# The sum of squares of four feed-forwards, as two matmuls of 128 tokens with two weight tiles between them

## The reference, cut to what matters

```python
def rms_norm(x, g):
    y = xf * lax.rsqrt(jnp.mean(xf * xf, axis=-1, keepdims=True) + NORM_EPS)
    return y * g
x = x + 0.5 * swiglu(rms_norm(x, ffn1_norm[l]), w_gate, w_up, w_down)   # silu(x @ w_gate) * (x @ w_up) @ w_down
```

## Time and profile before

| | |
|---|---|
| median of 3 runs | 1090.55 us (1090.24 to 1093.16) |
| the profiled execution's own time | 1091.57 us |
| its span, first to last instruction | 1089.7 us |
| TensorE matmuls busy | 1074.7 us (99%) |
| weight loads busy | 939.6 us (86%), beside the matmuls |
| VectorE, ScalarE, POOL busy | 782.0, 615.4, 186.5 us |
| mean granted TensorE clock | 0.995 |
| transfers | 200.02 MB, 184 GB/s on average |

### The profile page before, as it was taken

One profiled execution on the slowest core, in us unless ns is written; L12 is line 12 of the kernel. 1 busy time (PEld: TensorE's weight loads), 2 busy tenths in 40 slices (PEclk: granted clock), 3 DMA queues, 4 the chain that ended last, 5 costly groups with the idle time before them and its releaser, 6 DMA issues.

```text
span 1089.7 us, 17862 instructions
## 1 busy us (share of the span) xinstructions
PE 1074.7 (99%) x6282; PEld 939.6 (86%) x6282; DVE 782.0 (72%) x1110; ACT 615.4 (56%) x941; POOL 186.5 (17%) x199
## 2 busy tenths in 40 slices
PE   8999999999999999999999999999999999999997
PEld 6888888888788888888888888889988898888886
DVE  6866666798696666668666676787877769666664
ACT  7655544466675555447555445756655556555541
POOL 4411101030021111011111100233210022111100
PEclk9999999999999999999999999999999999999997
DMA  7755555554256555656555554655455646655551
GB/s 281 265 191 191 180 183 179 166 182 142 92 185 205 189 192 175 198 173 209 193 192 188 179 194 153 221 184 193 158 191 193 192 137 215 198 188 190 183 184 39
DMA packets 55571, 200.02 MB, mean 184 GB/s; under 512 B 6304, under 2 KB 6304, under 8 KB 55392
## 3 DMA queue, kind: packets, MB, share of 16 engines
q1 hardware_dynamic: 54576, 196.11, 54.9%
q0 software_dynamic: 512, 2.65, 0.6%
q10 hardware_dynamic: 432, 0.57, 0.2%
HBM read 198.26 MB, written 1.05 MB: 183 GB/s over the span
## 4 chain that ended last, share of the span: by engine, by line
PE 93%; DVE 5%; ACT 1%; DMA 1%; issue 0%; ACTq 0%; DVEq 0%
PE pair L1274 44%; PE pair L1275 22%; PE pair L1296 9%; PE pair L1298 5%; PE pair L1268 3%; PE pair L1270 3%; PE pair L1269 3%; DVE w_lo L790 2%; DVE x_hl L796 1%; DMA x<-x_in 1%; ACT qk_a L623 0%; PE pair L1637 0%; DVE x L807 0%; PE pair L1595 0%; ACT w_hi L429 0%
## 5 line engine op out<-in xcount | busy, mean ns | idle before, releaser
L790 DVE TENSOR_TENSOR w_lo<-w_raw,w_hi 128x1024 fp32r<-128x1024 f32 x369 | 463.1, 1262 | 230.6 <-ACT w_hi L429 229.9
L429 ACT ACTIVATE w_hi<-w_raw 128x1024 fp32r<-128x1024 f32 x369 | 386.1, 1056 | 236.4 <-PE pair L1275 195.4
L1274 PE MATMUL pair<-x_hl,w_hi 128*128 128x512 f32 x1408 | 493.2, 396 | 2.3 <-DVE x_hl L796 1.3
L1275 PE MATMUL pair<-x_hl,w_lo 128*128 128x256 f32 x1408 | 392.6, 279 | 0.0
L1274 PEld LDWEIGHTS pair<-x_hl,w_hi 128*128 128x128 f32 x1408 | 264.0, 187 | 66.1 <-issue 2.1
L1275 PEld LDWEIGHTS pair<-x_hl,w_lo 128*128 128x128 f32 x1408 | 265.2, 188 | 0.1
L1274 PE MATMUL pair<-wide,w_hi 128*128 128x512 f32 x704 | 245.4, 394 | 0.0
L1275 PE MATMUL pair<-wide,w_lo 128*128 128x256 f32 x704 | 196.2, 279 | 0.0
L1274 PEld LDWEIGHTS pair<-wide,w_hi 128*128 128x128 f32 x704 | 132.0, 187 | 30.8
L347 POOL TENSOR_TENSOR wide<-side,wide 128x256 fp32r<-128x256 f32 x88 | 86.4, 982 | 375.8 <-ACT wide L491 375.8
L1275 PEld LDWEIGHTS pair<-wide,w_lo 128*128 128x128 f32 x704 | 132.6, 188 | 0.0
(11 more groups left out here) (191 smaller groups left out, 1059.7 us busy)
## 6 DMA issues: line engine op xcount, KB each, us to landing
w_raw<-stream SPq DMA_DIRECT2D x369, 512.0 KB, 4.2
const<-const_in POOLq DMA_DIRECT2D x1, 1248.0 KB, 8.7
w_raw<-stream SPq DMA_DIRECT2D x4, 256.0 KB, 5.7
out<-x_sq SPq DMA_DIRECT2D x4, 256.0 KB, 2.6
rows<-rows_in POOLq DMA_DIRECT2D x1, 576.0 KB, 10.7
x<-x_in ACTq DMA_DIRECT2D x2, 256.0 KB, 5.7
x<-x_in SPq DMA_DIRECT2D x2, 256.0 KB, 6.8
sgu_w<-sgu_w_in POOLq DMA_DIRECT2D x1, 512.0 KB, 13.7
```

Source lines behind the costliest of these rows:

```text
L429: nc.scalar.activation(w_hi[:, slot, :], w_raw[:, slot, :], ACT.Copy).then_inc(w_hi_done, 1)
L790: nc.vector.tensor_tensor(w_lo[:, slot, :], w_raw[:, slot, :], w_hi[:, slot, :].bitcast(F32), ALU.subtract).then_inc(w_split, 1)
L1274: nc.tensor.matmul(dst, a_hi, b_hl.rearrange("p a s -> p (a s)"), start=first, stop=False, skip_group_check=True)
L1275: return nc.tensor.matmul(dst[:, 0:S], a_lo, b_hl[:, 0, :], start=False, stop=last, skip_group_check=True)
```

## The change

In the four feed-forwards `sum_squares` (one matmul of 256 tokens) becomes two matmuls of 128 tokens, each with the wait for `x_sq_added`. The first stands where the whole one stood, between blocks 3 and 4. The second stands in block 4 behind its first two tiles (before k = 2) and signals `sumsq_done`. Block 4 is written out for this, block 5 is a `wide_block` as it was in `chunk(2, 0)`, and the loop over chunks begins with 3. The mixers keep `sum_squares`. What is computed stays the same.

```diff
+            def sum_squares_half(p, t):
+
+                tok = slice(t * P, (t + 1) * P)
+                pe.wait_ge(x_sq_added, (KC - 1) * (p + 1))
+                return nc.tensor.matmul(bank[STAT[p]][:, tok], ones[:], x_sq[:, 0, tok], start=True, stop=True,
+                                        skip_group_check=True)
+
...
                 wide_block(n0 + 2, bank[6], x_hl)
                 wide_block(n0 + 3, bank[7], x_hl)
-                sum_squares(p)
+                sum_squares_half(p, 0)
+                pe.wait_ge(w_split, n0 + 5)
+                for k in range(KC):
+                    if k == 2:
+                        sum_squares_half(p, 1).then_inc(sumsq_done, 1)
+                    w = slice(k * P, (k + 1) * P)
+                    last = both(bank[0][:, :], w_hi[:, (n0 + 4) % RING, w], w_lo[:, (n0 + 4) % RING, w], x_hl[:, k, :, :],
+                                k == 0, k == KC - 1)
+                last.then_inc(w_used, 1)
+                wide_block(n0 + 5, bank[1], x_hl)
...
-                for f in range(2, LEAD):
+                for f in range(3, LEAD):
                     if f == 3:
                         pe.wait_ge(ms_done, p + 1)
-                    elif f >= 4:
+                    else:
                         pe.wait_ge(parts_added, FC * e + f - 3)
                     chunk(f, (f + 2) % 4)
```

## The result

| | before | after |
|---|---|---|
| median, 6 runs each | 1089.95 us (1086.7 to 1093.16) | 1100.76 us (1099.96 to 1101.87) |
| ratio | | 1.0107, interval 1.0091 to 1.0122 |
| span of the profiled execution | 1089.7 us | 1100.0 us |

The account below looks back on a forecast made before the run. TensorE's own stream, busy 1074.7 of 1089.7 us, was taken as the bound. The halves at +0.08 us and the waits at nothing gave 1091.65 us for the profiled execution, 1090.6 as median, range 1089.5 to 1093.0.

Parts of the forecast that it names:

- The step that failed: Total for the whole kernel: +0.08 us on the profiled execution's 1091.57 us, giving 1091.65, with a median of 1090.6.
- The bounds: Extra matmuls and loads of the four feed-forward sums: from below 0, from above 1.5 us if each shows a full load.
- The price of the halves: TensorE's stream at the split sums: two halves 0.446 us against 0.427, +0.02 us a call, +0.08 us for four feed-forwards.
- Rival (a): At the split sums, the weight loads are exposed: +1.5 us, 1092.1; chance 0.05.
- The rule of the Trainium skill: At the sums, a weight load overlaps matmuls in flight only where row groups differ; it would make the cost +0.85 us.
- The waits: Behind the sums: `ms` 0.72 us later, absorbed before the reciprocal; the later split of block 7 priced at nothing.
- Rival (b): The late sum passes through VectorE's `ms`, split and inverse root to TensorE in blocks 8 to 10: 1093.0; chance 0.04.
- The second wait: The second half's wait for `x_sq_added` in block 4 is already met when reached; put at nothing.
- the 0.03 for slower: Chance that the whole kernel measures slower, beyond the 0.3% (3.3 us) a measurement can tell from no change.
- an unseen mechanism: Besides (a) and (b) together, the only thing thought able to move the kernel's time past 3.3 us, on either side.

Follow-up runs that it names:

- eight tiles: Against the change: the second half stands behind all eight tiles of block 4 instead of two; 1100.38 us.
- the whole sum at `k == 6`: Against the change: both halves kept, then the whole sum once more four tiles behind the second half, which signals; 1088.73 us.
- the experiment with the wait alone: Against the change: whole sum in its old place, block 4 written out with the mid-block wait but no matmul there; 1090.19 us, ratio to before 0.9994.

## Why the prediction was wrong

**The step that failed** is the sum, "Sum: +0.08 us on the profiled execution's 1091.57 us". It adds the nanoseconds of the edited place and any new wait, and puts the spacing of the pairs behind the edit at nothing, with no more reason than that they are "the same matmuls in the same order". In its place the runs showed +6.67 ns in each of 1520 pairs between the sums, 10.1 us. The bounds and the rivals all lived at the edited place or in waits, so the range of 1089.5 to 1093.0 could not hold 1100.76.

**The price of the halves** was right: 0.22 us each was forecast and measured. Rival (a), the exposed loads, did not occur. The rule of the Trainium skill quoted there (page "TensorE: Matmul & The Clock Gate", Part 3, The mechanism), with that page's load time, would have asked for 0.107 us more for each load, an estimate. By that rule, the trace does not agree: a half with its two loads took 0.22 us. The same section of the Trainium skill also lets a load go ahead of running matmuls where it goes to the background weight buffer; with that sentence the trace is in keeping.

**The waits** were right too: `ms` 0.71 us later (0.72 forecast) and waiting 9.1 us for the sums (9.3 forecast), the root at the end of the table load, TensorE's wait for `w_lo` 1.0 us in total. Rival (b) did not occur; a sum delayed further, by 2.1 us with eight tiles, left the time where it was but for 0.3 us more of waits for `w_lo`, and with the whole sum at `k == 6` the kernel was fast.

**The second wait** at nothing: shown by the experiment with the wait alone.

**What the profile had shown.** The stretches of the kernel before read 397 pairs in 140 us in the first feed-forward (352.6 ns) and 492 in 170 (345.5 ns) in the second. I took "pairs start 0.35 us apart" from one spot, and the two values round to the same figure. The three runs, 1090.24 and 1090.55 and then 1093.16, were a step apart, and I read that as noise. The idea that an interruption sets a state of the stream was in no rival, and the 0.03 for slower was left for "an unseen mechanism".

**What stays open.** The cause is shown as far as this: the lost time lies in the spacing, and which pieces stand in the stream sets the spacing. Why the spacing has two values, and why a piece of 64 or 128 columns mostly leaves the slow one behind it while one of 256 mostly leaves the fast one, is not explained; the runs give the transitions, not the mechanism. The two spacings are 52 and 53 times 6.67 ns, and that is all that can be said. Nor is it shown what differs from run to run in one kernel. A last piece of 192 columns and four matmuls of 128 back to back were seen four times each, which is too few for a table.

## What to carry to other kernels

Where one engine runs a long regular stream, an edit can be worth more in the stream behind it than in its own place. So count the instructions in long stretches on both sides of the edit, to a part in a hundred, before pricing the edit alone. Runs that group in steps point to a state of the kernel rather than to noise, and the size of the step, divided by a count of instructions, helps to find which. A tight place with no wait in it is a risk for that state even if the wait would be only 60 ns, as at block 11 here.

## What the runs showed of the hardware that was not expected

- A stream of matmul pairs (fp32r, 512 columns then 256, each with its own 128x128 weight load) runs at one of two spacings, 346.7 or 353.3 ns a pair, at the same granted clock, and keeps it for some 500 pairs. Sixteen in a row of each kind take 347.5 ns a pair.
- An fp32 matmul between the pairs can change it: of 256 columns it left the fast spacing in 13 of 17 cases with no other piece shortly before it, and always when it met the fast one; of 64 or 128 columns, two tiles behind another piece, it left the slow one in 17 of 17. A piece of 128 columns that stood eight tiles or more from any other left the slow one in 6 of 8, and always (3 of 3) when it met the fast one.
- A stall at a wait changed it as well, in three of seven cases at block 11 of the first feed-forward, once with only 0.06 us.
- One fp32 matmul of the program (two recorded) takes 0.43 us of the stream with 256 columns, and 0.22 us with 128.
